# Relative-position bias tiles read back in descending rows from a replicated table, and attention probabilities scaled on VectorE before a true transpose

## The reference

```python
step_dist = qi + n_steps - kj
bias = rel_bias[t5_bucket(jnp.maximum(step_dist, 0) * dilation)]     # (q, k, head)
logits = jnp.einsum('brnqhe,brnkhe->brnhqk', qb, kw) * scale + bias  # masked outside the window
p = jnp.exp(logits - max(logits)); denom = jnp.sum(p, axis=-1)
o = jnp.einsum('brnhqk,brnkhe->brnqhe', p, vw) / denom
```

## Time and profile before

| | us |
|---|---|
| device time, median of 3 runs | 1348.53 |
| device time, lowest and highest run | 1346.73 and 1348.92 |
| span of the profiled execution | 1347.1 |
| PE busy in it | 1285.3 (95%) |
| DVE busy | 358.0 (27%) |
| ACT busy | 245.2 (18%) |
| POOL busy | 6.6 (0%) |

### The profile page before, as it was taken

How to read it: one execution, slowest core, us unless ns; L and a number is a source line. 1 busy time by engine, 2 the same in 40 slices (tenths; PEclk the granted TensorE clock), 3 DMA queues, 4 the chain that set the end, 5 groups by cost and what they waited for, 6 DMA issues and landing times.

```text
span 1347.1 us, 19047 instructions
## 1 busy us (share of the span) xinstructions
PE 1285.3 (95%) x7598; PEld 680.9 (51%) x7599; DVE 358.0 (27%) x677; ACT 245.2 (18%) x313; POOL 6.6 (0%) x13
## 2 busy tenths in 40 slices
PE   5999999999699999999999999999999999999995
PEld 5999887998533333333333333333333433333332
DVE  4434653523711112112111121121111211211112
ACT  4444543421400001100000011000000110000001
POOL 0000000000100000000000000000000000000000
PEclk9999999999799999999999999999999999999998
DMA  8745434833389999999999999999999999999990
GB/s 290 238 155 183 164 126 170 346 141 125 141 342 420 419 418 419 418 419 416 416 417 419 418 419 418 418 418 416 417 418 418 418 417 417 414 412 415 411 402 40
DMA packets 99188, 461.54 MB, mean 343 GB/s; under 512 B 9569, under 2 KB 9626, under 8 KB 66362
## 3 DMA queue, kind: packets, MB, share of 16 engines
q1 hardware_dynamic: 95928, 457.83, 84.4%
q10 hardware_dynamic: 2802, 1.74, 0.5%
q0 software_dynamic: 432, 1.59, 0.3%
HBM read 460.07 MB, written 1.07 MB: 342 GB/s over the span
## 4 chain that ended last, share of the span: by engine, by line
PE 84%; DMA 6%; SPq 4%; ACT 2%; issue 2%; DVE 1%; DVEq 0%; ACTq 0%
PE ps L850 27%; PE ps L874 15%; PE ps L892 8%; DMA w_ring<-in_w 6%; PE ps L844 4%; PE ps L661 3%; PE ps L664 3%; PE ps L663 3%; PE ps L834 3%; PE ps L867 2%; PE ps L791 2%; PE ps L668 2%; PE ps L670 2%; PE ps L669 2%; SPq L325 2%
## 5 line engine op out<-in xcount | busy, mean ns | idle before, releaser
L850 PE MATMUL ps<-w_ring,A_W 128*64 128x512 f32 x2048 | 446.2, 592 | 1.9 <-DMA w_ring<-in_w 1.8
L850 PEld LDWEIGHTS ps<-w_ring,A_W 128*64 128x64 f32 x2048 | 146.9, 137 | 295.8 <-issue 285.0
L874 PE MATMUL ps<-w_ring,A_W 128*64 128x512 f32 x1024 | 226.1, 592 | 0.0
L591 ACT ACTIVATE A_W<-A_W 128x512 f32<-128x512 f32 x32 | 20.2, 630 | 756.4 <-DVE A_W L1213 756.4
L874 PEld LDWEIGHTS ps<-w_ring,A_W 128*64 128x64 f32 x1024 | 88.4, 137 | 131.3 <-issue 131.3
L1213 DVE TENSOR_SCALAR A_W<-ps 128x512 f32<-128x512 f32 x32 | 22.1, 692 | 436.2 <-PE ps L850 436.2
L892 PE MATMUL ps<-A_W 128*128 128x512 f32 x264 | 121.4, 603 | 1.3 <-DVE A_W L1233 1.3
L943 DVE TENSOR_TENSOR w_parts<-w_ring,w_parts 128x1024 fp32r<-128x1024 f32 x76 | 92.6, 1225 | 109.6 <-ACT w_parts L475 105.9
L661 PE MATMUL ps<-hT_hi,w_parts 128*128 128x256 f32 x384 | 110.2, 287 | 2.0 <-ACT hT_hi L494 2.0
L664 PE MATMUL ps<-hT_hi,w_parts 128*128 128x256 f32 x384 | 109.4, 285 | 0.0
L663 PE MATMUL ps<-hT_lo,w_parts 128*128 128x256 f32 x384 | 109.3, 285 | 0.0
(11 more groups left out here) (194 smaller groups left out, 872.3 us busy)
## 6 DMA issues: line engine op xcount, KB each, us to landing
w_ring<-in_w SPq DMA_DIRECT2D x384, 1024.0 KB, 17.2
w_ring<-in_w_in SPq DMA_DIRECT2D x38, 1024.0 KB, 7.1
w_ring<-in_w_ret_branch SPq DMA_DIRECT2D x2, 2048.0 KB, 12.3
A_W<-in_w_out SPq DMA_DIRECT2D x1, 2560.0 KB, 13.2
xb<-in_x SPq DMA_DIRECT2D x4, 512.0 KB, 3.7
A_QK<-in_w_att_branch SPq DMA_DIRECT2D x1, 2048.0 KB, 10.0
w_ring<-bias_scratch POOLq DMA_DIRECT2D x1, 1536.0 KB, 11.8
A_W<-in_w_out SPq DMA_DIRECT2D x1, 1536.0 KB, 8.4
```

The lines of the kernel that those rows point to most:

```text
L850: mm = pe.matmul(o, XT[:, k, :], w1_ring[:, k, c * HALF:(c + 1) * HALF], start=False, stop=(k == KC - 1))
L874: mm = pe.matmul(ps[CAP * c:CAP * c + CAP, 7, :], lhs, w2_ring[:, q, c * HALF:(c + 1) * HALF], start=False, stop=(n == FQ - 1))
```

## The change

The table is stored to DRAM 128 times per head, so that `bias_scratch` is 12 x 128 x 384 numbers instead of 12 x 384. With that, one read with a step of 383 numbers between partitions, from number 127 on, puts into partition p the 256 numbers that start at number 127 - p: copy p of the row, one number further back each time. It lands directly in `toep`. The flipped identity, the six matmuls on PE, the six copies on ACT and their two semaphores are gone.

For the probabilities, DVE multiplies them in place by 1/sum (two instructions, 3x128 and 3x256 numbers per partition) instead of writing two diagonals, and PE transposes the nine blocks with the identity as a transpose proper. `diag` is gone, and with it ACT's wait at group 13.

```diff
-    early = np.concatenate([rot, cos, sin, ident[::-1]], axis=1)
+    early = np.concatenate([rot, cos, sin], axis=1)
...
-        toep_up = w2_flat[:, 4096:7168]
...
-        diag = gr[:, 1, :].rearrange("p (b q) -> p b q", b=8)
...
-        scratch = nc.dram_tensor("bias_scratch", (N_ATT_HEADS, 384), F32, kind="Internal").ap()
+        scratch = nc.dram_tensor("bias_scratch", (N_ATT_HEADS, P, 384), F32, kind="Internal").ap()
...
-            pool.dma_start(scratch, tab_sb).then_inc(s_tab, 16)
+            pool.dma_start(scratch, tab_sb.rearrange("h (a c) -> h a c", a=1).broadcast_to([N_ATT_HEADS, P, 384]))\
+                .then_inc(s_tab, 16)
             pool.wait_ge(s_tab, 16)
-            pool.dma_start(toep_up.rearrange("p (h c) -> p h c", h=N_ATT_HEADS),
-                           bass.AP(scratch.tensor, 0, [[1, P], [384, N_ATT_HEADS], [1, T]])).then_inc(s_toep, 16)
+            pool.dma_start(toep,
+                           bass.AP(scratch.tensor, P - 1, [[383, P], [384 * P, N_ATT_HEADS], [1, T]])).then_inc(s_toep, 16)
...
                 elif g < 15:
-                    if g == 13:
-                        act.wait_ge(s_pt, SLOTS * GROUPS)
                     act.activation(gr[:, :, (g - 13) * HALF:(g - 12) * HALF], ps[:, b:b + 2, :], ACT.Silu).then_inc(s_proje, 1)
...
-            for n in range(6):
-                act.wait_ge(s_flip, n + 1)
-                act.activation(toep[:, 2 * n:2 * n + 2, :].rearrange("p h c -> p (h c)"), bank(4 + n % 4), ACT.Copy)\
-                    .then_inc(s_flipe, 1)
...
-            def turn_bias_tiles():
...
-                pe.wait_ge(s_diag, 2 * (s + 1))
+                pe.wait_ge(s_norm, TT * (s + 1))
                 for g in range(GROUPS):
                     for n, (tile, k) in enumerate(((0, 0), (1, 0), (1, 1))):
-                        mm = pe.matmul(ps[:, 4 + g, n * P:(n + 1) * P], probs[:, s % 2, g, (tile + k) * P:(tile + k + 1) * P],
-                                       diag[:, 2 * s + tile, :], start=True, stop=True)
+                        mm = pe.transpose(ps[:, 4 + g, n * P:(n + 1) * P],
+                                          probs[:, s % 2, g, (tile + k) * P:(tile + k + 1) * P], ident)
                     mm.then_inc(s_pt, 1)
...
-            turn_bias_tiles()
...
-            dve.wait_ge(s_flipe, 6)
+            dve.wait_ge(s_toep, 16)
...
-                for t in range(TT):
-                    dve.tensor_scalar(diag[:, 2 * s + t, :], ident, rden[:, 2 * s + t:2 * s + t + 1], None, ALU.mult)\
-                        .then_inc(s_diag, 1)
+                for t, keys in enumerate((slice(0, P), slice(P, 384))):
+                    dve.tensor_scalar(probs[:, s % 2, :, keys], probs[:, s % 2, :, keys],
+                                      rden[:, 2 * s + t:2 * s + t + 1], None, ALU.mult).then_inc(s_norm, 1)
```

More of the change, by code:

```diff
@@ L154, in hybrid_block_kernel @@
         qk = A_QK[:, 0:8192].rearrange("p (g c t) -> p g c t", g=QK_GROUPS, c=4)
-        early = A_QK[:, 8192:8192 + 768]
-        rot, cosT, sinT, flip = early[:, 0:P], early[:, P:P + T], early[:, P + T:P + 2 * T], early[:, P + 2 * T:2 * P + 2 * T]
+        early = A_QK[:, 8192:8192 + 640]
+        rot, cosT, sinT = early[:, 0:P], early[:, P:P + T], early[:, P + T:P + 2 * T]
         gateA = A_QK[:, 0:2048].rearrange("p (c t) -> p c t", c=KC)
@@ L226, in hybrid_block_kernel @@
         s_toep = sem("bias_tiles_loaded")
-        s_flip = sem("bias_tiles_turned")
-        s_flipe = sem("bias_tiles_stored")
         s_win = [[sem(f"w_in_loaded{b}_{half}") for half in range(2)] for b in range(W_BUFS)]
@@ L255, in hybrid_block_kernel @@
         s_exp = sem("exps_done")
-        s_diag = sem("diag_ready")
+        s_norm = sem("probs_normed")
         s_pt = sem("probs_transposed")
@@ L675, in rotate_pairs @@
                 pe.wait_ge(s_proje, 8)
-                pe.wait_ge(s_flipe, 6)
                 for i in range(2):
```

## The result

| | before | after |
|---|---|---|
| median of the runs on one chip, us | 1347.63 (1346.56 to 1348.92, 4 runs) | 1357.26 (1355.29 to 1359.67, 4 runs) |
| span of the profiled execution, us | 1347.1 | 1354.8 |

The changed kernel is slower: the ratio of the times is 1.0073, 95% interval 1.0058 to 1.0087. The forecast was 1338.7 us, so 18.6 us are missing. The chain of the page says where they are. Before, its shares were those of the earlier trace rows; now they are

The account below looks back on a forecast made before the run. PE was taken as the bound, busy 95% of the span, with PE and DMA full in the expert stretch. Gains 5.15 + 1.22 + 3.43 = 9.80 us, clock 1.7 - 1.7, took 1348.53 to 1338.7 us; range 1335.8 to 1341.5.

Parts of the forecast that it names:

- Making the tiles by DMA: POOL's store and read-back before attention: store 17.7 us, tiles there at about 61 us, 79 us of cover, cost zero.
- The third rival: Transposes give nothing in slots 1 and 2 (1339.9 us), or projection loads are 2 us late (1340.7 us); chance 0.13.
- The rival on the store: Too few DMA engines serve the store, so DVE waits for the tiles and the kernel is slower; chance 0.03.
- The sign of my own warning: In the projection stretch: the forecast is wrong if ACT waits for `in_w_in` between 35 and 60 us.
- Turning the bias tiles: Between groups 4 and 5, PE loses the 12 passes of L639 with no idle time in them; gain 5.15 us.
- Slots: Attention slots 0 to 3: cheaper transposes and ACT's earlier table load gain 0, 0.61, 0.61 and 3.43 us.
- The clock in slot 3: With PE's wait cut from 2.67 to about 0.3 us, no clock fall is expected behind it; 1.7 us gained.
- The clock in slot 0: PE's wait grows from 1.19 to 2.21 us, so a clock fall is expected behind it; 1.7 us lost.
- The rival without it: No clock fall behind slot 0's wait; the gain is 11.5 us, giving 1337.0 us; chance 0.27.
- DVE's scaling: In each attention slot, two in-place scalings take 0.42 + 0.62 us, keeping DVE busy 0.5 us longer; cost zero.
- The expert stretch: From 345 us on, PE and DMA are both full for 963 us; savings made earlier arrive whole at the end.

Follow-up runs that it names:

- e3: Changed kernel, but the table is stored to DRAM once and copied 128 times from DRAM to DRAM; 1338.05 us, ratio 0.9925 to the kernel before.
- e5: Kernel before plus an unused 2304 KB store on POOL, read from all 128 partitions of another tile; 1347.98 us, beside 1349.47 before.
- e4: Kernel before plus an unused 2304 KB store on POOL, read from the table's partitions 0 to 11; 1367.29 us, beside 1349.47 before.
- e9: Kernel before plus an unused 2304 KB store from the table's 12 partitions, issued by ACT instead of POOL; 1354.87 us, one run.
- e10: Changed kernel with 16 copies of each row instead of 128 (288 KB), read back by eight DMAs; 1338.0 us, ratio 0.9935 to the kernel before.
- e1: Kernel before with only the second part: probabilities scaled on DVE and truly transposed, bias tiles made as before; 1341.95 us, ratio 0.9959.
- e7: Kernel before plus an unused 2304 KB store on POOL, read from partitions 0 to 11 of another tile; 1365.27 us, beside 1347.47 before.
- e8: Kernel before plus an unused 2304 KB store on POOL, read from partitions 0, 8, ... 88 of another tile; 1352.45 us, beside 1347.47 before.
- e6: Changed kernel with DVE's wait on `g_col` and the eight router scalings moved behind the projection; 1353.93 us, one run.
- e2: Changed kernel with the diagonals and their matmuls put back, so only the new bias tiles remain; 1362.6 us, ratio 1.0109 to the kernel before.

## Why the prediction was wrong

Step by step:

- **Making the tiles by DMA** is the step that failed: "I take zero, with 2 us as the upper end." It cost about 19.2 us (1357.26 - 1338.05, the changed kernel against e3). Two numbers in it were wrong. The store was sized as 17.7 us by the pace of the read of 1536 KB, the nearest row of the profile; it took 35.9. That read writes to all 128 partitions and takes its data from DRAM, while the store takes them from 12 partitions: e5, with the same bytes from 128 partitions, took 10.5 us. The larger error is the next sentence, that a load at half pace is still in time. The loads did not go at half pace but at a fifth, 34.5 us for 6.4, because engines that the store holds for 0.7 us a packet are seldom free for SP's packets of 0.09. e4 shows the loss with the store alone, and e9 a smaller one with smaller packets. The third rival had named this very delay, but at 2 us, without a row for it.
- **The rival on the store** had the place wrong. I asked how long DVE could wait for the tiles, found 79 us of cover and gave a loss a chance of 0.03. The tiles were there at 66.36 + 11.3 = 78 us, and DVE first used them at 159.9 in this run. The loss was on the loads beside the store, and I had bounded that by a guess at their pace, not by a row. The rule that I had cited there from the Trainium skill, page "DMA: Bandwidth & Descriptors", section on why a DMA increments its semaphore by 16, fits the packet records, with at most 12 of the store's packets at once (13 for moments). It was no protection: the engines were many and slow. (In that rival half of 25 GB/s is 189 us and not 191; nothing rests on it.) The sign of my own warning, ACT waiting for `in_w_in` between 35 and 60 us, is what the trace shows.
- **Turning the bias tiles**, 5.15 us: right. From the matmul of the bias table to the rotation matmuls behind group 9 it is 97.5 us before, and 92.4 in e3 and in e10, 5.1 less.
- **Slots**: 0, 0.61, 0.61 and 3.43 forecast, 4.65 in all, with waits of 2.21, 0.41, 0.41 and 0.3. The waits were 2.22, 0.25, 0.25 and 0.35, within 0.16 us each. From scores to scores the changed kernel gains 0.58, 0.47 and 3.23 us in slots 1 to 3 (16.36, 16.36 and 16.43 us for 16.94, 16.83 and 19.66), 4.3 in all. Right.
- **The clock in slot 3**: right. The fall of the earlier trace rows is gone with the wait, and `ret_scores` takes 2.62 us (221.97 to 224.59) where it took 4.28, 1.7 less, as forecast. With the slots, the stretch from group 9 to the branches gives 5.9 us (after, and e1 too: 148.6 us both against 154.5); 4.65 + 1.7 would be 6.35.
- **The clock in slot 0**: wrong. I expected a fall behind a wait of 2.21 us. In four traces (after, e1, e3, e10) the granted clock is 1.00 there. The rival without it was the right one for this part, at 11.5 us in sum. The traces bear it out: without the stall the two stretches give 5.1 + 5.9 = 11.0 us, while e3's median is 10.2 below the kernel before and e10's 9.5; in e3's trace 0.9 us of the difference lies ahead of the table, which starts at 31.0 and not 30.1. So it is luck in part that e3 and e10 come out next to the forecast's 9.8, which had 1.7 us too little here.
- **DVE's scaling**: 1.22 us a slot (485 + 734 ns) for 1.04 forecast, hidden as said.
- **The expert stretch** passes on what comes: from the branches to the end it is 1065.0 us before, 1064.0 after and 1064.6 in e3.

One reading of the prediction goes too far as well. It held that this trace disagrees with the rule that it cites from the Trainium skill, page "TensorE: Matmul & The Clock Gate", part 4. It looked at 347 to 349 alone. The windows of the kernel before, a few us on, have the fall:

```profile
351.00:352.00 1.00, 1.00 (x12) 1.00 (x11) 1.00 (x2) 0.11 (x1) 0.00 (x0) 1.00 1.08 459
352.00:353.00 1.00, 1.00 (x9) 1.00 (x9) 1.00 (x2) 0.95 (x1) 0.00 (x0) 0.73 0.98 410
353.00:354.00 1.00, 1.00 (x6) 1.00 (x6) 1.00 (x2) 0.91 (x1) 0.00 (x0) 0.50 0.99 418
```

Ahead of the fall stand a wait of 1.38 us, the 16 transposes, another wait of 1.36 us and 2 us of the router's small matmuls. So the row of 1.00 settles nothing about transposes. Nor did the fall in slot 0 come, which the prediction called sure by that rule.

So two terms of the sum failed. The fall in slot 0 was 1.7 us too much. The cost of making the tiles, set to zero, was 19.2 us, twice the rest with the other sign. What is shown: the source in 12 neighbouring partitions makes the store slow (e4 and e7 against e8, e5 and e3), the store makes the loads late (e4, e6), and without that the change is worth 0.7% (e3, e10). What stays open: whether a packet of one row on POOL's queue would behave as on ACT's, which was not tried; and e4 to e9 are single runs, which is enough for 5 us and more and not for the last microsecond.

## What to carry to other kernels

A DMA has two prices: its own slack, and what its packets take from the queues beside it; the second has to be worked out even where the first is zero. Before a broadcast leaves SBUF, count the partitions that it is read from, and look how near they lie: twelve neighbours gave 70 GB/s and took the engines with them, and the same rows out of DRAM (e3) or an eighth of the copies (e10) made PE wait for nothing. A pace taken from another row of a profile holds only if that row has the same kind of source.

## What the runs showed of the hardware

- A store of 2304 KB from SBUF took 33.8 to 35.9 us from 12 neighbouring partitions, 20.8 from 12 that lie eight apart, and 10.5 from 128; the copy from DRAM to DRAM took 14.6. One packet of three rows took 0.67 us from neighbours (e7), 0.34 or 0.18 from every eighth partition (e8), 0.20 on the mean from 128 (e5) and 0.18 from DRAM (e3).
- The same access pattern made packets of 4608 bytes on POOL's queue and of 1536 on ACT's. The first left SP's queue 1.39 MB in 36 us, the second 3.75.
- With 9 transposes right ahead of it, a wait of 2.22 us left the granted clock at 1.00 in four traces; in the kernel before, a wait of 2.67 us behind matmuls was followed by 0.61, and in e8 a wait of 3.7 us ahead of 57.67 by 0.71 (60 to 62 us). Whether the transposes, the length or what PE did earlier makes the difference, no run here separates.
- The wait of 2.01 us at the start stands in every trace, and the granted clock behind it does not follow it: its mean from 10 to 20 us is 0.90 in the kernel before and in e10, and 1.00 in the changed kernel and in e1, e2 and e3. It is no certain mark of a fall, and I had used it as one of the two neighbours from which I took a fall in slot 0.
